# Mixer values projected in feature layout and transposed on TensorE; three slots for split weights; another order in the second half of the output projection

## The reference, cut to what matters

```python
z = xn @ p["w_in"] + p["b_in"]
(gla_q, gla_k, gla_v, ..., ml_q, ml_k, ml_v, ml_o, ml_i, ml_f, gate_a, gate_b, gate_c) = jnp.split(z, ...)
y_a = gla_branch(gla_q, gla_k, gla_v, gla_r, gla_a, p) @ p["w_br_gla"]
y_b = dsa_branch(dsa_cq, dsa_ckv, idx_k, idx_w, p, t5_table) @ p["w_br_dsa"]
y_c = mlstm_branch(ml_q, ml_k, ml_v, ml_o, ml_i, ml_f, p) @ p["w_br_ml"]
mix = sigmoid(gate_a) * y_a + sigmoid(gate_b) * y_b + sigmoid(gate_c) * y_c
h = h + rms_norm(mix @ p["w_out"], p["g_post_mix"])
xn = rms_norm(h, p["g_pre_mlp"])
h = h + rms_norm(square(relu(xn @ p["w_up"])) @ p["w_down"], p["g_post_mlp"])
```

## Time and profile before

| | |
|---|---|
| runs of the kernel (3) | median 1262.3 us, 1262.03 to 1263.04 |
| profiled execution, own time | 1262.05 us |
| its span, first to last instruction | 1260.1 us |
| mean granted TensorE clock | 0.999 of full |
| busy: TensorE / its weight loads | 1252.5 us (99%) / 1028.6 us (82%) |
| busy: GpSimd / VectorE / ScalarE | 771.8 (61%) / 629.7 (50%) / 392.7 us (31%) |
| DMA | 120.08 MB, mean 95 GB/s |

### The profile page before, as it was taken

How to read it: one execution, slowest core, us unless ns; L and a number is a source line. 1 busy time by engine, 2 the same in 40 slices (tenths; PEclk the granted TensorE clock), 3 DMA queues, 4 the chain that set the end, 5 groups by cost and what they waited for, 6 DMA issues and landing times.

```text
span 1260.1 us, 17438 instructions
## 1 busy us (share of the span) xinstructions
PE 1252.5 (99%) x6561; PEld 1028.6 (82%) x6564; DVE 629.7 (50%) x1115; ACT 392.7 (31%) x810; POOL 771.8 (61%) x914
## 2 busy tenths in 40 slices
PE   9999999999999999999999999999999999999998
PEld 8866887677899899888899987887888888888886
DVE  4368887642276786835446773342511112333434
ACT  5343555533013333333024343312511111221322
POOL 8746430225574753758775556784876676888882
PEclk9999999999999999999999999999999999999999
DMA  6846200323331321322443333522333333232221
GB/s 176 253 123 212 68 2 25 80 56 94 84 84 51 84 68 51 84 68 84 118 117 77 87 90 100 195 89 85 84 101 101 86 99 108 93 101 84 100 84 67
DMA packets 167433, 120.08 MB, mean 95 GB/s; under 512 B 11367, under 2 KB 145613, under 8 KB 167350
## 3 DMA queue, kind: packets, MB, share of 16 engines
q1 hardware_dynamic: 160612, 107.79, 29.7%
q10 hardware_dynamic: 6738, 11.18, 2.7%
HBM read 114.71 MB, written 9.62 MB: 99 GB/s over the span
## 4 chain that ended last, share of the span: by engine, by line
PE 99%; ACT 0%; DVE 0%; issue 0%; DVEq 0%; ACTq 0%
PE GP L1874 46%; PE GP L1910 9%; PE PA L1910 9%; PE GP L1889 7%; PE GP L1871 6%; PE PA L2075 3%; PE GP L2137 3%; PE PA L2175 1%; PE PA L2112 1%; PE PA L2293 1%; PE GP L2368 1%; PE GP L1956 1%; PE PA L2045 1%; PE PA L2285 1%; PE PA L2076 1%; PE GP L1881 1%
## 5 line engine op out<-in xcount | busy, mean ns | idle before, releaser
L624 POOL TENSOR_TENSOR wlo<-wraw,whi 128x256 fp32r<-128x256 f32 x708 | 563.9, 827 | 14.8
L620 POOL TENSOR_SCALAR whi<-wraw 128x1024 fp32r<-128x1024 f32 x177 | 201.0, 1135 | 449.2 <-PE GP L1874 226.6
L1874 PE MATMUL GP<-xh,whi 128*128 128x512 f32 x352 | 144.8, 411 | 0.0
L1874 PE MATMUL GP<-xh,wlo 128*128 128x512 f32 x352 | 139.0, 395 | 0.0
L1874 PE MATMUL GP<-xl,whi 128*128 128x512 f32 x352 | 138.8, 394 | 0.0
L1816 DVE TENSOR_TENSOR ul<-U,uh 128x512 fp32r<-128x512 f32 x64 | 65.3, 1055 | 109.4 <-ACT uh L1158 109.4
L1874 PE MATMUL GP<-nh,whi 128*128 128x512 f32 x240 | 95.1, 396 | 0.0
L1874 PE MATMUL GP<-nl,whi 128*128 128x512 f32 x240 | 95.1, 396 | 0.0
L1874 PE MATMUL GP<-nh,wlo 128*128 128x512 f32 x240 | 95.1, 396 | 0.0
L1820 DVE SCALAR_TENSOR_TENSOR U<-GP,rrow 128x512 f32<-128x512 f32 x32 | 22.1, 692 | 141.7 <-PE GP L1874 140.3
L1874 PEld LDWEIGHTS GP<-xh,whi 128*128 128x128 f32 x352 | 66.3, 188 | 16.0 <-issue 1.5
(11 more groups left out here) (426 smaller groups left out, 2770.5 us busy)
## 6 DMA issues: line engine op xcount, KB each, us to landing
wraw<-in_w_in SPq DMA_DIRECT2D x75, 512.0 KB, 3.9
wraw<-in_w_up SPq DMA_DIRECT2D x32, 512.0 KB, 4.0
wraw<-in_w_down SPq DMA_DIRECT2D x32, 512.0 KB, 3.5
line_rows<-bias_line SPq DMA_DIRECT2D x8, 655.0 KB, 5.2
table<-line_rows SPq DMA_DIRECT2D x4, 1024.0 KB, 5.7
wraw<-in_w_br_dsa SPq DMA_DIRECT2D x8, 512.0 KB, 4.3
wraw<-in_w_br_gla SPq DMA_DIRECT2D x8, 512.0 KB, 4.0
wraw<-in_w_br_ml SPq DMA_DIRECT2D x8, 512.0 KB, 4.0
```

Of the source, the lines that this page charges most:

```text
L620: nc.gpsimd.tensor_scalar(hi, src, 1.0, 1.0, ALU.mult, ALU.mult).then_inc(hi_done, 1)
L624: part = nc.gpsimd.tensor_tensor(lo[:, at:to], src[:, at:to], hi[:, at:to].bitcast(FP32), ALU.subtract)
L1874: ins = mm(ps[0:t.m, 0:SEQ], wt[:, s0, w], av, start=st, stop=sp_)
```

## The change

The values of both mixers become ordinary feature tiles (`both`, all 528 tokens, two chunks per head). ScalarE evacuates each with its bias into `vT` (the bias rows now come with the other bias columns). A tile of the new kind T transposes it in five pieces on TensorE, and VectorE or ScalarE copies the result to `vh` and `vm`, the places that the mixers read. Tile M, `xm` and `vb` go. NHL is 3. In the second half of the output projection chunk 0 is multiplied for all tokens first, and chunks 1 to 3 for each block in turn. The bias rows are loaded by 20 DMAs in place of 22.

```diff
@@ -52,7 +52,7 @@
-NHL = 4
+NHL = 3
@@ -160,17 +160,8 @@
-    def values(name, c0):
-        c = [chunk("w_in", c0, P), chunk("w_in", c0 + P, P)]
-        assert c[0] % 2 == 0
-        tile(name + "A", c, 0, kind="V", off=0)
-        tile(name + "B", c, 0, kind="V", off=2)
-        tile(name + "M", c, 2, kind="VT" if name[0] == "m" else "VM")
-    def pad():
-        if len(chunks) % 2:
-            chunks.append(None)
+    def turned(name, v):
+        tile(f"{name}T{v}", [], 0, kind="T")
@@ -210,7 +201,11 @@
+        if h == 1:
+            turned("gv0", 0)
+        if h == 1:
+            turned("gv0", 1)
@@ -222,12 +217,12 @@
-    def all_values(name, c0):
-        pad()
-        values(name, c0)
+    def value(name, c0, h, v):
+        feature(f"{name}{h}{v}", "w_in", c0 + (2 * h + v) * P, both=True)
-    all_values("gv0", C_GV)
+    value("gv", C_GV, 0, 0)
+    value("gv", C_GV, 0, 1)
@@ -235,22 +230,34 @@
-            all_values(f"gv{h + 1}", C_GV + (h + 1) * DV)
+            value("gv", C_GV, h + 1, 0)
+            value("gv", C_GV, h + 1, 1)
+            turned(f"gv{h + 1}", 0)
+            turned(f"gv{h + 1}", 1)
-    all_values("mv0", C_MV)
+    value("mv", C_MV, 0, 0)
+    value("mv", C_MV, 0, 1)
-        if h + 1 < HEADS:
+        more = h + 1 < HEADS
+        if more:
+        else:
+            gates("tc", C_GATE + 2 * D, 0, 1)
+        if h == 0:
+            turned("mv0", 0)
+        turned(f"mv{h}", 1)
+        if more:
+            value("mv", C_MV, h + 1, 0)
+            turned(f"mv{h + 1}", 0)
+            value("mv", C_MV, h + 1, 1)
-            gates("tc", C_GATE + 2 * D, 0, 2)
-        if h + 1 < HEADS:
-            all_values(f"mv{h + 1}", C_MV + (h + 1) * DV)
+            gates("tc", C_GATE + 2 * D, 1, 2)
@@ -926,18 +929,37 @@
+            def value_in(name, h, v):
+                if h:
+                    act.wait_ge(gemm_done, tl[f"{name}{h - 1}T{v}"].val)
+                t = tl[f"{name}{h}{v}"]
+                nc.scalar.activation(two(vT[:, v, :]), halves(ready(f"{name}{h}{v}")), ACT.Identity,
+                                     bias=cc(name, 2 * h + v)).then_inc(gfree[t.slot], 1)
+            def values_copied(h):
+                ps = ready(f"gv{h}T1")
+                nc.scalar.activation(vh[:, h % 2, :, P:DV], ps[:, 0:SEQ].rearrange("p (t n) -> p t n", t=QT), ACT.Copy)
+                nc.scalar.activation(vm[0:META, h % 2, P:DV], ps[0:META, SEQ:SEQ + P], ACT.Copy).then_inc(gfree[tl[f"gv{h}T1"].slot], 1)
+            value_in("gv", 0, 0)
+            value_in("gv", 0, 1)
+                    values_copied(h)
+                if h == 0:
+                    values_copied(0)
@@ -954,10 +976,12 @@
+                if not last:
+                    value_in("gv", h + 1, 0)
+                if not last:
+                    value_in("gv", h + 1, 1)
-                    whole("gv3M")
@@ -1044,6 +1067,8 @@
+            value_in("mv", 0, 0)
+            value_in("mv", 0, 1)
@@ -1081,13 +1106,15 @@
+                    value_in("mv", h + 1, 0)
+                if more:
+                    value_in("mv", h + 1, 1)
-            whole("mv3M")
@@ -1384,18 +1409,12 @@
-            dve.wait_ge(ld_a, 48)
-            def values(name, h, part):
-                if part < 2:
-                    t = tl[f"{name}{h}{'AB'[part]}"]
-                    ps = ready(f"{name}{h}{'AB'[part]}")
-                    tt(vh[:, h % 2, 2 * part:2 * part + 2, :], ps[:, 0:2 * DV].rearrange("p (t n) -> p t n", t=2),
-                       vb[:, h * DV:(h + 1) * DV].unsqueeze(1).broadcast_to([P, 2, DV]), ALU.add).then_inc(gfree[t.slot], 1)
-                    return
-                ps = ready(f"{name}{h}M")
-                dve.wait_ge(f16_ok, 2)
-                stt(vm[0:2 * META, h % 2, :], vb[0:2 * META, h * DV:(h + 1) * DV], first16[:, :], ps[0:2 * META, 0:DV], ALU.mult, ALU.add).then_inc(gfree[tl[f"{name}{h}M"].slot], 1)
+            def values(name, h, v):
+                ps, c = ready(f"{name}{h}T{v}"), slice(v * P, (v + 1) * P)
+                nc.vector.tensor_copy(vh[:, h % 2, :, c], ps[:, 0:SEQ].rearrange("p (t n) -> p t n", t=QT))
+                nc.vector.tensor_copy(vm[0:META, h % 2, c], ps[0:META, SEQ:SEQ + P]).then_inc(gfree[tl[f"{name}{h}T{v}"].slot], 1)
@@ -1562,6 +1578,8 @@
+                if h == 0:
+                    values("gv", 0, 0)
@@ -1588,8 +1606,7 @@
-                    values("gv", h + 1, 1)
-                    values("gv", h + 1, 2)
+                    values("gv", h + 1, 0)
@@ -1726,16 +1740,16 @@
-            dve.wait_ge(ld_v, 16)
-            for part in range(3):
-                values("mv", 0, part)
+                else:
+                    values("mv", 0, 0)
+                values("mv", h, 1)
@@ -1752,9 +1766,6 @@
-                if more:
-                    for part in range(1, 3):
-                        values("mv", h + 1, part)
@@ -1872,22 +1883,13 @@
-                elif t.kind in ("V", "VM", "VT"):
-                    s0 = chunks[t.chunks[0]]["hl"]
-                    if t.kind != "V":
-                        for k in range(KT):
-                            w = slice(k * P, (k + 1) * P)
-                            mm(ps[0:2 * META, 0:DV], xm[:, k, :], whi[:, s0:s0 + 2, w], start=(k == 0), stop=False)
-                            ins = mm(ps[0:2 * META, 0:DV], xm[:, k, :], wlo[:, s0:s0 + 2, w], start=False, stop=(k == KT - 1))
-                    tokens = [] if t.kind != "V" else [0, 1] if part is None else [part]
-                    first = 0 if name[0] == "m" else META
-                    for i in tokens:
-                        tok = slice(first + (t.off + i) * P, first + (t.off + i + 1) * P)
-                        o_ = ps[:, i * DV:(i + 1) * DV]
-                        for k in range(KT):
-                            for p_, (at_, wt) in enumerate([(xh, whi), (xh, wlo), (xl, whi)]):
-                                ins = mm(o_, at_[:, k, tok], wt[:, s0:s0 + 2, k * P:(k + 1) * P],
-                                         start=(k == 0 and p_ == 0), stop=(k == KT - 1 and p_ == 2))
+                elif t.kind == "T":
+                    v, first = int(name[4]), 0 if name[0] == "m" else META
+                    few = slice(SEQ, ALL) if name[0] == "m" else slice(0, META)
+                    evacuated(name[0:3] + name[4])
+                    for i in range(QT):
+                        nc.tensor.transpose(ps[:, i * P:(i + 1) * P], vT[:, v, first + i * P:first + (i + 1) * P], ident[:, :])
+                    ins = nc.tensor.transpose(ps[0:META, SEQ:SEQ + P], vT[:, v, few], ident[:, :])
@@ -2209,13 +2211,17 @@
                     if h + 1 < HEADS:
                         gemm(f"{kind[0:2]}{h + 1}{kind[2:]}", part)
                     elif kind != "gg":
-                        gemm({"gq": "ta0", "gk": "ta1", "gvA": "ta2", "gvB": "ta3", "gvM": "ta4"}[kind], part)
+                        gemm({"gq": "ta0", "gk": "ta1", "gv0": "ta2", "gv1": "ta3", "gvT0": "ta4"}[kind], part)
                 evacuated(f"gq{h}", f"gk{h}")
                 nxt("gq")
                 if h:
                     squares(h - 1)
+                else:
+                    gemm("gv0T0")
                 nxt("gk")
+                if h == 0:
+                    gemm("gv0T1")
                 level(h, 0)
                 nxt("gg")
                 level(h, 1)
@@ -2238,19 +2244,21 @@
-                nxt("gvB", 0)
+                nxt("gv1", 0)
-                evacuated(f"gv{h}A", f"gv{h}B", f"gv{h}M")
+                evacuated(f"gv{h}T0", f"gv{h}T1")
-                nxt("gvB", 1)
-                nxt("gvM")
+                nxt("gv1", 1)
+                nxt("gvT0")
+                if h + 1 < HEADS:
+                    gemm(f"gv{h + 1}T1")
@@ -2298,7 +2304,7 @@
-                        gemm({"mq": "tc0", "mk": "tc1", "mvA": "tc2", "mvB": "tc3", "mvM": "tc4"}[kind], part)
+                        gemm({"mq": "tc0", "mk": "tc1", "mv0": "tc2", "mvT0": "tc3", "mv1": "tc4"}[kind], part)
@@ -2310,22 +2316,25 @@
+                else:
+                    gemm("mv0T0")
+                gemm(f"mv{h}T1")
-                nxt("mvA")
+                nxt("mv0")
-                evacuated(f"mv{h}A", f"mv{h}B", f"mv{h}M")
+                evacuated(f"mv{h}T0", f"mv{h}T1")
-                nxt("mvB")
-                nxt("mvM")
+                nxt("mvT0")
+                nxt("mv1")
@@ -2369,8 +2378,9 @@
                                  start=(hf == 0 and k == 0 and p_ == 0), stop=(hf == 1 and k == KT - 1 and p_ == 2))
                 return ins
+            token_gemm("out", 0, 1, mixed(0), last=True)
             for t in range(QT):
-                for n_ in range(4):
+                for n_ in range(1, 4):
                     ins = token_gemm("out", n_, 1, mixed(n_), tiles=[t])
                     if t == QT - 1 and n_ < 3:
                         ins.then_inc(gemm_done, 1)
```

(36 more changed lines are left out.)

21 lines of the change are left out of this document (5 added, 16 removed).

## The result

The changed kernel takes 1268.05 us (median of 5, 1267.46 to 1268.43) against 1262.63 (1262.03 to 1263.45) for the kernel before on the same chip: ratio 1.004, 95% interval 1.003 to 1.0051. That is 5.4 us slower, where I had forecast 0.8 us slower, and 1.25 us above the top of my range. The profiled execution took 1268.1 us with a span of 1266.4.

The account below looks back on a forecast made before the run. An unbroken queue of TensorE instructions was taken to bound the kernel. Terms -4.4 + 0.3 + 2.3 + 2.6 = +0.8 on the profiled 1262.05 gave 1262.9, as a median 1263.0 us; 8-in-10 range 1259.6 to 1266.8.

Parts of the forecast that it names:

- Three slots, mo1: Gemm mo1, among the query latents: TensorE waits for its split, released later with three slots; 2.3 us lost.
- Output projection: Second half: the fourth w_out chunk's late split, VectorE falling behind and up1's split; 2.6 us lost together.
- Hand-over of gk1: GLA: gk1 needs gq1's PSUM slot with only five transposes between; 0.3 us lost, once.
- Value part: Values of all 8 heads on TensorE: feature gemms and transposes replace tiles A, B and M; 4.4 us saved.
- Hand-overs of mLSTM: Value evacuations, transposes and copies in mLSTM heads are covered: 0 lost, at most 1 us at each of six places.
- My section on the slots: GpSimd splits chunk r only after gemm r-3, not r-4; late splits priced at mo1, 2.3 us lost.
- My sign for this part: TensorE's chain between 345 and 745: about 4 us shorter, no wait over 0.5.
- the upper extreme of my sum: Whole kernel, terms at their slow bounds: -2.8 + 1 + 4.1 + 4.0 = +6.3 us.
- Rival C: mLSTM value hand-overs stall, ScalarE late for the transposes: 1 us at six places, 1269; chance 0.10.
- Rival A: Clock falls in new gaps at mo1 or output stage: 1.7 us per fall, 1264.8 or 1266.5; chance 0.22.
- Rival B: The slots are no bound at mo1 or w_out; the 4.4 us saved stand alone: 1258.0; chance 0.12.
- rival D: Value part saves nothing, transposes costing as much as tile M, 14.9 in place of 8.8: 1269; chance 0.03.

Follow-up runs that it names:

- e1: The changed kernel with four slots for split chunks (NHL 4) in place of three: 1263.16 us.
- e3: The kernel before with only the new order of the output projection's second half, four slots, values as before: 1263.61 us, ratio 1.0003.
- e5: Value form alone (four slots, old output order), GpSimd's split into a head's first value chunk's slot held until the second value gemm is done: 1259.44 us.
- e10: e5 with 960 bytes per partition left unused where xm stood, so xh, xl and stage tiles have the addresses of before: 1259.73 us.
- e7: e5 with VectorE's copy of the next mLSTM head's first value tile also moved behind head_sums: 1259.66 us.
- e9: The changed kernel with three slots and its output order, plus the held split of e5: 1264.58 us, ratio 1.0014.
- e6: Value form alone (four slots, old output order), VectorE's copy of the next mLSTM head's first value tile moved behind head_sums: 1271.95 us, ratio 1.0073.

## Why the prediction was wrong

By its own steps, with what the traces show for each:

- **Three slots, mo1** (+2.3): 2.3, with the wait of 2.1 at 93.12, released by the split that starts at 88.56. Right.
- **Output projection** (+2.6): +2.3 up to up0 and the wait of 0.3 for up1's split behind it. The fourth chunk's split cost 1.6 where I had 1.3, VectorE's lateness (nl) 0.7 where I had 1.1 (e1, e3), up1's split 0.3 where I had 0.2. The waits are right; that the sum is too is in part luck, as the errors cancel.
- **Hand-over of gk1** (+0.3): the wait for qg, 0.3. Right.
- **Value part** (-4.4): 0.8 to 1.6 too much. e5 saves 3.3 in all, e10, with the addresses of before, 2.5, both with the 0.3 of gk1 in it; by my terms it was 4.1. I had priced all 16 feature gemms with the 5.83 us of gk0. Some take more here: two in 11.95, so 5.97 each, in the first GLA head (11.94 in e10, so it is not the addresses), and up to 5.94 in mLSTM. Why is open. Chain of the changed kernel:
```profile
349.69 11.95 PE GP L1882 x96
...
662.64 5.94 PE GP L1882 x48
```
- **Hand-overs of mLSTM** (0, bounds 0 and 6). **This is the step that failed.** I wrote that the copy in front of `conv_mul` delays the denominator by 1.5 us and that 5.83 + 2.9 us of gemms behind it cover that. The stage lost 3.1 us (e5 against the changed kernel: 1.37 and 1.71 in heads 1 and 2). The sentence checks the added delay against the cover and not the chain's slack. In the kernel before rso was done at 718.12 for scores at 719.29, so 1.2 us were left:
```profile
717.49 0.63 ACT L644 ACTIVATE rso<-rso 128x512 f32<-128x512 f32 x1
```
```profile
719.29 1.53 PE PA L2285 x4
```
  The change also took 1.1 us of cover away (tile B and M after `recalled`, 7.5 us, gave way to 6.4), but that is not what cost: with the split held rso is done at 715.84 for scores at 717.47 (e5), 1.6 us of slack, copies and all. The split takes more than that: from the start of yl to the end of rso it is 19.2 us in the changed kernel and 16.4 in e5. Of the 2.8 between them 1.6 are slack, and what is left, with some 0.2 for the pipeline to fill again, is head 1's 1.37. Head 2 loses 0.6 of its 1.71 only with three slots (34.11 in e1). These 2.8 are neither the copies, which both kernels have, nor ScalarE: they start with GpSimd's split, moved beside VectorE's two-input work by the chunk's earlier release. My section on the slots asked of each split whether it comes too late; nowhere did I ask whether one now comes earlier, and beside what. With the split held, copies and shorter cover cost nothing (e5, e7). My sign for this part, a chain some 4 us shorter between 345 and 745 with no wait over 0.5, failed with it: there is a wait of 1.2 at 721.51. And the upper extreme of my sum, +6.3, counted 1 us for the hand-overs, where their own bounds allow 6; with these it is +11.3.
- **Rival C** (hand-overs stall, 1269) named the stage and came nearest in time, but with ScalarE late for the transposes, which no trace shows.
- **Rival A** (the clock) did not happen in the profiled execution. It did in e9 at the same gap, for the 1.7 us that I had priced, in three runs of 11, and in e6. The median of 1268.05 holds none of it: its run has a mean granted clock of 1.000. The page that I cited for it (the Trainium skill, TensorE: Matmul & The Clock Gate, "HAM oscillation") warns of waits for data between groups of matmuls; e9 agrees, the changed kernel's own trace does not.
- **Rival B** (no bound by the slots) is refuted by e1, **rival D** by the transposes: ten take about 1.1 us, as priced.

Sum over the steps, by the table: e5 against the kernel before is -3.3, of which -2.5 is the value part with gk1's 0.3 in it (e10) and -0.7 the addresses (+0.4 in the attention, -0.7 in the up projection, -0.4 in all others together). The changed kernel against e5 is +8.3: mo1 2.3, the slowed mLSTM heads 3.1, the output projection 2.3, the up projection 0.4 with up1's split in it, and 0.2 in two others. Together +5.0, against my +0.8: 3.1 of the miss of 4.2 are the slowed heads, 0.8 the value part. The medians differ by 5.4; the other 0.4 is in no stretch.

## What to carry to other kernels

A buffer's release is an event with two sides: releasing it earlier starts its next producer earlier, and the question is what that producer then runs beside. Before a wait is priced by the work that covers it, read the slack of the whole chain from the two rows that meet (here rso's end and the scores' start); only what exceeds that slack costs, and lost cover counts like added delay. Where moving a copy later seems free, look for who waits for the buffer that it empties.

## What the hardware showed that I had not expected

- A gap of 2.07 us in dense TensorE work left the clock at full in the changed kernel's profiled execution and dropped it to the 1.2 GHz level in that of e9, for 1.7 us in all. By the mean granted clock it fell in three of e9's 11 runs. The two gaps of 3.66 us in e6 dropped it both times (0.995 in all five runs), its gap of 1.12 us did not.
- The same matmuls take 0.2 to 1% more or less with the SBUF addresses of their operands: 2.86 against 2.83 us for 12, 181.6 against 182.3 for the up projection. One shift helps one stage and costs another; which addresses suit which stage is open.
- The first 26 matmuls took from 4.53 to 5.83 us in these executions, whatever the kernel. So 1.3 us of a difference between two spans can be the start alone.
- Five GpSimd subtractions on one scratch tile slowed yl to 2.12 us, a split of a weight chunk to 2.66, from 1.29. A VectorE copy out of PSUM beside a split kept its 0.69.
